# A decoder trunk on one core: the order of work in the state-space scan stage

## The reference

```
lam_bar = exp(lam * dt); b_bar = ((lam_bar - 1) / lam) * (b_re + i b_im)   # 32 groups, 64 states, 16 channels
bu = einsum('bsgc,gpc->bsgp', u, b_bar)
h  = scan over time of  h[t] = lam_bar * h[t-1] + bu[t]
y  = einsum('bsgp,gcp->bsgc', h, c).real + d_skip * u;  y = gelu(y)
compress(z, j): blocks of 32 tokens (stride 16) of z + cmp_pos[j], gelu(zb @ cmp_w1[j] + cmp_b1[j]) @ cmp_w2[j]
```

## Time and profile before

| | |
|---|---|
| median of 3 runs | 1891.24 us |
| profiled execution | 1887.98 us, span 1886.2 us |
| PE busy | 1795.3 us (95%) |
| DVE, ACT, POOL busy | 926.4, 660.6, 182.2 us |
| end of a2_1 on PE, layer 1 | 70.52 us |
| end of POOL's table, layer 1 | 84.0 us |
| first L691 of batches 0 to 3, layer 1 | 118.80, 138.63, 160.30, 177.16 us |
| the same, layer 2 | 1050.70, 1070.49, 1092.50, 1109.32 us |
| DVE, per batch | blocks 1.5, `input_mats` 4.2, `output_mats` 4.6, skips 0.3, scan 5.9 us |
| DVE, hidden gelu with its tanh | 103.71 to 105.88 us, the three operations ahead of the tanh 1.3 us |
| `load_z2(0, 1)`, the first group | issued from 55.08 to 57.64 us |

### The profile page before, as it was taken

The page is one execution under the profiler, slowest core; times in us unless marked ns, Lnnn a source line. Parts: engine busy times, 40 slices in busy tenths (PEclk is TensorE's granted clock), DMA queues, the critical chain, the costliest instruction groups (busy, mean ns, idle before and its releaser), DMA issues.

```text
span 1886.2 us, 25936 instructions
## 1 busy us (share of the span) xinstructions
PE 1795.3 (95%) x9640; PEld 1440.8 (76%) x9640; DVE 926.4 (49%) x1465; ACT 660.6 (35%) x1156; POOL 182.2 (10%) x325
## 2 busy tenths in 40 slices
PE   6899999999989999999988999999999899999997
PEld 6677766778877888888766777767788688888886
DVE  4786576444444444422348956754443444444223
ACT  4332655522234222221253235654222432222112
POOL 3601060000000000000044010600000000000000
PEclk9999999999999999999999999999999999999999
DMA  7334112123222333322243341211333133333222
GB/s 259 103 99 110 57 51 62 58 89 100 89 74 74 98 94 98 98 90 90 79 171 94 107 106 55 62 35 56 90 93 97 56 94 96 100 94 96 90 89 78
DMA packets 65590, 171.11 MB, mean 91 GB/s; under 512 B 14480, under 2 KB 26768, under 8 KB 64736
## 3 DMA queue, kind: packets, MB, share of 16 engines
q1 hardware_dynamic: 40192, 140.53, 24.2%
q10 hardware_dynamic: 22208, 14.16, 2.9%
q0 software_dynamic: 3104, 15.25, 2.6%
HBM read 160.18 MB, written 7.08 MB: 89 GB/s over the span
## 4 chain that ended last, share of the span: by engine, by line
PE 83%; DVE 8%; ACT 4%; DVEq 3%; issue 1%; DMA 1%; ACTq 0%
PE ps L503 18%; PE ps L505 17%; PE ps L504 17%; PE ps L542 6%; PE ps L544 5%; PE ps L543 5%; PE ps L759 2%; PE ps L772 2%; PE ps L785 2%; PE ps L533 1%; DVE ta L1266 1%; DVE wlo L1260 1%; PE ps L641 1%; ACT rta L929 1%; DMA xt<-xin 1%
## 5 line engine op out<-in xcount | busy, mean ns | idle before, releaser
L503 PE MATMUL ps<-xh,whi 128*128 128x512 f32 x1312 | 523.3, 399 | 18.7 <-DVE wlo L1260 11.5
L505 PE MATMUL ps<-xh,wlo 128*128 128x512 f32 x1312 | 514.5, 392 | 0.0
L504 PE MATMUL ps<-xl,whi 128*128 128x512 f32 x1312 | 514.2, 392 | 0.0
L1260 DVE TENSOR_TENSOR wlo<-raw,whi 128x1024 fp32r<-128x1024 f32 x264 | 328.4, 1244 | 340.8 <-ACT whi L901 331.1
L901 ACT ACTIVATE whi<-raw 128x1024 fp32r<-128x1024 f32 x264 | 278.1, 1053 | 369.3 <-PE ps L544 246.8
L503 PEld LDWEIGHTS ps<-xh,whi 128*128 128x128 f32 x1312 | 248.6, 190 | 72.3 <-DVE wlo L1260 13.2
L505 PEld LDWEIGHTS ps<-xh,wlo 128*128 128x128 f32 x1312 | 248.3, 189 | 53.2
L504 PEld LDWEIGHTS ps<-xl,whi 128*128 128x128 f32 x1312 | 248.8, 190 | 49.6
L542 PE MATMUL ps<-whi,hh 128*128 128x512 f32 x352 | 137.7, 391 | 5.1 <-DVE wlo L1260 5.1
L544 PE MATMUL ps<-whi,hl 128*128 128x512 f32 x352 | 137.1, 389 | 0.0
L543 PE MATMUL ps<-wlo,hh 128*128 128x512 f32 x352 | 137.0, 389 | 0.0
(11 more groups left out here) (338 smaller groups left out, 2437.7 us busy)
## 6 DMA issues: line engine op xcount, KB each, us to landing
raw<-wstream SPq DMA_DIRECT2D x264, 512.0 KB, 3.5
w<-w1s POOLq DMA_DIRECT2D x4, 2048.0 KB, 12.3
sm<-smalls POOLq DMA_DIRECT2D x2, 1084.0 KB, 5.4
xt<-xin ACTq DMA_DIRECT2D x4, 512.0 KB, 10.6
scratch_u<-pa ACTq DMA_DIRECT2D x8, 256.0 KB
toep<-scratch_k ACTq DMA_DIRECT2D x4, 512.0 KB
scratch_y<-y ACTq DMA_DIRECT2D x8, 256.0 KB
toep_b<-scratch_k ACTq DMA_DIRECT2D x4, 512.0 KB
```

The costliest lines, as they stand in the source:

```text
L503: pe.matmul(ps[:, bank, :], wh, hi[:, k, :], start=first and i == 0, stop=False)
L504: pe.matmul(ps[:, bank, :], wh, lo[:, k, :], start=False, stop=False)
L505: m = pe.matmul(ps[:, bank, :], wl, hi[:, k, :], start=False, stop=last and i == len(blocks) - 1)
L1260: dve.tensor_tensor(wlo[:, c % 2, :], raw[:, c % 2, :], whi[:, c % 2, :].bitcast(f32), SUB).then_inc(lo_ready, 1)
```

## The change

`bch` holds the input blocks of all four batches (it lies where `gqt` was), made once by `input_blocks`; `skip` holds all skip matrices, made once. `s5_mats` is split on PE and ACT into the turn (`vmat` to `vt`) and the kernels (`bch`, `wmat` to `kam`), with a semaphore `vmat_ready` of its own; the turn of batch j+1 goes ahead, while the kernels of batch j+1 come after `s5_outputs(j)` and a slab, and are followed by one slab before `s5_outputs(j+1)`. PE does a2_3 and the hidden turns before the first turn and kernels. DVE adds the positions before it makes any matrix; ACT issues the second `load_z2` before `a2_out(0)`, and each split ahead of the stores and loads of u. The same matmuls are done in both kernels.

```diff
-    bch = more("bch", [P, 2, 4, SC])
+    bch = place("bch", at, [P, 2, GP, SC])          # at gqt
-    skip = place("skip", ys_at + 1024, [SC, 8, SC])
+    skip = place("skip", ys_at + 1024, [SC, SG, SC])
# PE
-                def s5_mats(b, j):
+                def s5_turn(b, j):
                     if j:
-                        pe.wait_ge(ka_copied, b)
-                    pe.wait_ge(mats_ready[j % 2], l * 2 + (j // 2 + 1))
+                        pe.wait_ge(vt_ready, b)
+                    pe.wait_ge(vmat_ready, b + 1)
...
+                def s5_kernels(b, j):
+                    if j:
+                        pe.wait_ge(ka_copied, b)
+                    pe.wait_ge(mats_ready[j % 2], l * 2 + (j // 2 + 1))
...
-                pe.wait_ge(vtok_ready, l + 1)
-                s5_mats(l * 4, 0)
+                a2_slab(3)
                 pe.wait_ge(qgate_tanh, l + 1)
                 pe.wait_ge(hid_copied, l + 1)
-                a2_slab(3)
                 for i in range(2):                    # hidden turns, L712
...
+                s5_turn(l * 4, 0)
+                pe.wait_ge(vtok_ready, l + 1)
+                s5_kernels(l * 4, 0)
                 b1_slab(0)
...
                 s5_states(l * 4, 0)
+                s5_turn(l * 4 + 1, 1)
                 b1_slab(1)
-                s5_mats(l * 4 + 1, 1)
                 for j in range(3):
                     s5_outputs(l * 4 + j, j)
+                    b1_slab(2 * j + 2)
+                    s5_kernels(l * 4 + j + 1, j + 1)
                     s5_states(l * 4 + j + 1, j + 1)
-                    b1_slab(2 * j + 2)
                     if j < 2:
+                        s5_turn(l * 4 + j + 2, j + 2)
                         b1_slab(2 * j + 3)
-                        s5_mats(l * 4 + j + 2, j + 2)
# ACT
                 a2_split(0)
+                load_z2(1, 0)
                 a2_out(0)
+                a2_split(1)
                 store_u(0)
-                load_z2(1, 0)
-                a2_split(1)
...
                 a2_out(1)
+                a2_split(2)
                 load_u(0)
                 store_u(1)
-                a2_split(2)
                 a2_out(2)
+                a2_split(3)
                 load_u(1)
                 store_u(2)
-                a2_split(3)
...
                 a2_out(3)
-                load_u(2); store_u(3); b1_split(1); store_k(l * 4, 0)
                 act.wait_ge(hid_psum, l + 1)          # bias
...
+                b1_split(1)
+                s5_turned(l * 4)
                 act.wait_ge(gelu_arg, l * 5 + 1)      # tanh
...
-                load_u(3); load_toep(l * 4, 0)
+                s5_kernels(l * 4); load_u(2); store_u(3); store_k(l * 4, 0)
                 b1_out(0)
                 b1_split(2)
+                load_toep(l * 4, 0); s5_turned(l * 4 + 1); load_u(3)
                 b1_out(1)
                 b1_split(3)
-                s5_mats(l * 4 + 1); store_k(l * 4 + 1, 1)
                 for j in range(3):
                     s5_outputs(b, j)
                     store_y(b, j)
-                    load_toep(b + 1, j + 1)
                     if j < 2:
                         b1_out(2 * j + 2)
                         b1_split(2 * j + 4)
+                    else:
+                        query_out(0, OQ0, 0)
+                        split_hi(hl_, OQ0 + 2)
+                    s5_kernels(b + 1)
+                    store_k(b + 1, j + 1)
+                    if j < 2:
+                        s5_turned(b + 2)
+                    load_toep(b + 1, j + 1)
+                    if j < 2:
                         b1_out(2 * j + 3)
                         b1_split(2 * j + 5)
-                        s5_mats(b + 2); store_k(b + 2, j + 2)
-                query_out(0, OQ0, 0)
-                split_hi(hl_, OQ0 + 2)
# DVE
+                def input_blocks():                   # all 16 columns of coef at once
+                    t1, t2 = ta[:, 0:256]..., tb[:, 0:256]...
+                    cmul(bch[:, 0, :, :], bch[:, 1, :, :], bc(coef[:, 0, :], 2, SC), bc(coef[:, 1, :], 2, SC), ...)
...
                 a2_lo(0)
-                input_mats(l * 4, 0)
+                add_positions(1)
                 a2_lo(1)
-                gq ...; for j in (1, 0): positions
+                add_positions(0)
                 a2_lo(2)
+                gq ...
+                input_blocks()
+                input_mats(l * 4, 0)
                 output_mats(l * 4, 0)
                 a2_lo(3)
-                skips(0); add_skip(l * 4); input_mats(l * 4 + 1, 1)
+                hidden_gelu()                         # with skips() ahead of its wait for the tanh
+                add_skip(l * 4, 0)
                 b1_lo(1)
-                gelu(...); output_mats(l * 4 + 1, 1)
+                input_mats(l * 4 + 1, 1)
+                scan(l * 4, 0)
...
                 b1_lo(2)
-                scan(l * 4, 0); b1_lo(3); input_mats(l * 4 + 2, 2); skips(1); add_skip(l * 4 + 1); output_mats(l * 4 + 2, 2)
                 for j in range(3):
+                    output_mats(l * 4 + j + 1, j + 1)
+                    b1_lo(2 * j + 3)
+                    if j < 2:
+                        input_mats(l * 4 + j + 2, j + 2)
+                    add_skip(l * 4 + j + 1, j + 1)
+                    b1_lo(2 * j + 4)
                     scan(l * 4 + j + 1, j + 1)
-                    b1_lo(2 * j + 4)
-                    if j == 0: input_mats(l * 4 + 3, 3)
-                    if j == 1: output_mats(l * 4 + 3, 3)
-                    if j < 2: b1_lo(2 * j + 5); skips(j + 2); add_skip(l * 4 + j + 2)
```

More of the change, by code:

```diff
@@ L1025, in load_u, with s5_turned @@
                     act.dma_start(u8s[i][:, :, :], scr_u[i].rearrange("c g t n -> t (c g) n")).then_inc(u8_in[i], 16)
[L1027 removed]
+                def s5_turned(b):
                     act.wait_ge(vt_psum, b + 1)
@@ L1030, in s5_mats, with s5_kernels @@
                        .then_inc(vt_ready, 1)
+                def s5_kernels(b):
                     act.wait_ge(ka_psum, b + 1)
@@ L1114, in _ @@
                 x.then_inc(hid_biased, 1)
+                b1_split(1)
+                s5_turned(l * 4)
                 act.wait_ge(gelu_arg, l * 5 + 1)
                 act.activation(hgt[:, :, :], hgt[:, :, :], ACT.Tanh, scale=GELU_B).then_inc(gelu_tanh, 1)
-                load_u(3)
-                load_toep(l * 4, 0)
+                s5_kernels(l * 4)
+                load_u(2)
+                store_u(3)
+                act.wait_ge(k_zeroed, 64)
+                store_k(l * 4, 0)
                 b1_out(0)
                 b1_split(2)
+                load_toep(l * 4, 0)
+                s5_turned(l * 4 + 1)
+                load_u(3)
                 b1_out(1)
                 b1_split(3)
-                s5_mats(l * 4 + 1)
-                store_k(l * 4 + 1, 1)
                 for j in range(3):
@@ L1521, in _ @@
                     x.then_inc(z_ready, 1)
+                a2_lo(0)
+                add_positions(1)
+                a2_lo(1)
+                add_positions(0)
                 a2_lo(2)
+                dve.wait_ge(qgate_tanh, l + 1)
+                dve.tensor_scalar(gq[:, :, :].rearrange("p t c -> p (t c)"), gq[:, :, :].rearrange("p t c -> p (t c)"), 1.0, 0.5, ADD, MUL)
+                input_blocks()
+                input_mats(l * 4, 0)
                 output_mats(l * 4, 0)
                 a2_lo(3)
-                skips(0)
-                add_skip(l * 4)
-                input_mats(l * 4 + 1, 1)
                 def b1_lo(i):
@@ L1553, in scan, with hidden_gelu @@
                           [x.rearrange(v3, g=4) for x in temps]).then_inc(h_ready, 1)
+                def hidden_gelu():
+                    y, t = hid[:, :, :], hgt[:, :, :]
+                    dve.wait_ge(hid_biased, l + 1)
+                    tt(t, y, y, MUL)
+                    dve.drain()
+                    dve.tensor_scalar(t, t, GELU_A, 1.0, MUL, ADD)
+                    dve.drain()
+                    tt(t, t, y, MUL).then_inc(gelu_arg, 1)
+                    skips()
+                    dve.wait_ge(gelu_tanh, l * 5 + 1)
+                    dve.scalar_tensor_tensor(t, t, 1.0, y, ADD, MUL).then_inc(hid_ready, 1)
+                hidden_gelu()
+                add_skip(l * 4, 0)
                 b1_lo(1)
-                dve.wait_ge(hid_biased, l + 1)
-                gelu(hid[:, :, :], hgt[:, :, :], l * 5).then_inc(hid_ready, 1)
-                output_mats(l * 4 + 1, 1)
+                input_mats(l * 4 + 1, 1)
+                scan(l * 4, 0)
                 dve.wait_ge(kc_psum, l + 1)
@@ L1567, in _ @@
                 b1_lo(2)
-                scan(l * 4, 0)
-                b1_lo(3)
-                input_mats(l * 4 + 2, 2)
-                skips(1)
-                add_skip(l * 4 + 1)
-                output_mats(l * 4 + 2, 2)
-                for j in range(3):
-                    scan(l * 4 + j + 1, j + 1)
-                    b1_lo(2 * j + 4)
-                    if j == 0:
```

(11 more changed lines are left out.)

50 lines of the change are left out of this document (15 added, 35 removed).

## The result

The changed kernel takes 1925.9 us (median of 4 runs, 1924.6 to 1928.5), the kernel before 1890.6 in the same job (4 runs, 1888.0 to 1892.6): ratio 1.0188, 95% interval [1.0174, 1.0201]. The prediction was 1881.4, range 1871 to 1896. It was wrong in sign and outside its range. The profiled execution took 1924.6 us with a span of 1922.8, against 1886.2 before.

What follows compares the result with a forecast made beforehand. PE, busy 95% of the span, bounds the kernel, so only its stalls count: 28.1 us removed less 18.2 of new waits gives 9.9 gained, 1878.1 from the profiled run, named as 1881.4 us; range 1871 to 1896 (8 in 10).

Steps and rivals of the forecast that it cites:

- the front: Start of the scan stage: position sums and z2 earlier remove the 4.9 us `wlo` wait and half clock, 7.5 us.
- the hidden products: Front of the stage: hidden matmuls follow the third slab at 76.1 us, their sums ready by about 73.2, so no stall.
- the first kernels: Ahead of the first kernels: a new wait of 1.1 us for output matrices that DVE ends at 91.3.
- the sum of removed stalls: PE's waits and half clock in the scan stage: 13.9 us in layer 1, 14.2 in layer 2, 28.1 in all.
- the first outputs: First output group L691 of layer 1: expected to start near 108 us instead of 118.8.
- 0.5 for the turn: Before the loop: PE asks for input_mats(1) at 100.6, DVE ends it at 101.1; a 0.5 us wait (0 to 1.5).
- 0.3 for kc: Ahead of the first outputs: scan and kc end at 108.0, PE comes free at 107.8; a 0.3 us wait.
- the mechanism of the loop: Batches 1 to 3: the Toeplitz chain through DRAM ends after PE reaches the outputs, 2.4 us wait three times per layer.
- 1.46 + 2.6: Toeplitz chain after the kernels end: the store is issued 1.46 us later and lands in 2.6, then the load starts.
- I take 6.0: Toeplitz load of 512 KB: assumed to land in 6.0 us, between bounds of 3.5 and 9.7.
- the new waits: Scan stage, per layer: 1.1+0.5+0.3+3x2.4 = 9.1 us, both layers 18.2.
- rival (b): Ahead of L691, batches 1 to 3: waits from about 3 us lower the clock, 1.5 us more each; 1897, chance 0.16.

Runs made afterwards that it cites:

- e5_kernels_earlier: Changed kernel with the kernels of batch j+1 put ahead of the slab and of outputs j; 1863.2 us, ratio 0.9857 to the kernel before.
- e6_half_load: Changed kernel loading half the rows of every Toeplitz block (512 instead of 1024), each used twice, so half the data is left out; 1888.0 us, ratio 0.9984.
- e7_raw_later: Changed kernel with DVE's low-part split of block 2j+4 behind the scan of batch j+1, so the raw load starts later; 1921.2 us, ratio 1.0164.
- e1_front_only: Changed kernel with its front kept and the batch loop in the order of before, kernels one batch ahead; 1882.2 us, ratio 0.9973.
- e9_front_scan_first: e1_front_only with the scan of batch 0 moved ahead of the output matrices of batch 1 on DVE; 1887.1 us, ratio 0.9986.
- e2_filled_wait: Changed kernel with 18 large matmuls, results unread, filling PE's wait ahead of outputs 1 to 3; 1900.5 us, ratio 1.0056.
- e3_wait_then_slab: Changed kernel with the wait for Toeplitz load and scan ahead of slab 2j+2, and the outputs behind that slab; 1926.0 us, ratio 1.0195.
- e8_small_fill: Changed kernel with 34 small matmuls of the outputs' size, results thrown away, ahead of outputs 1, 2 and 3; 1921.1 us, ratio 1.0172.

## Why the prediction was wrong

**Right: the front.** The third slab has no wait and a full clock; the hidden products start at 76.35 (predicted 76.1, before 83.72); the first kernels wait 1.40 for `wmat` (predicted 1.1); the `upool`, `wmat_b`, `pa` and scan waits are gone. `e5_kernels_earlier` bears out the sum of removed stalls. Off by a little: the first outputs start at 109.23, not 108; in place of 0.5 for the turn and 0.3 for kc there is one wait of 1.40 for the first Toeplitz load (2.81 in layer 2). The sum had followed that load nowhere: its store was issued at 96.87, right behind a u store of 256 KB, and landed only as the load went out, at 102.61.

**Right: the mechanism of the loop.** The chain kernels, copy, skip sum, store, load became the last thing that the outputs wait for, and the first half of its working held: the kernels of batch 1 end at T = 120.61, where the states begin, PE is free for outputs 1 at T+7.65 (predicted 7.75) and starts them at T+11.77, and the load was issued at T+3.9 (predicted 1.46 + 2.6 = 4.1).

**Wrong: "I take 6.0" for the load.** It takes 7.1 to 7.8 us. I priced the bytes at the 169 GB/s of the earlier trace rows, a window that lies behind the y store as well, and added 2.0 us from a store of 64 KB. `e6_half_load` puts the load's own bytes at 105 to 114 GB/s and the rest at 2.8 to 2.9 us, and `e7_raw_later` shows that the raw load beside it counts for 0.4 us on average. The waits were 3.9 to 4.1 in layer 1 instead of 2.4. With the waits ahead of outputs 0 the new waits are 14.9 us in layer 1 and 15.2 in layer 2, where the sum had 9.1 each: 11.9 us too few.

**Wrong, and larger: the clock behind the waits.** The sum has no term for it, and rival (b), whose mechanism it is, priced it at 1.5 us per wait and "from about 3 us on", from one slab. Behind outputs it is half of 11.5, 10.2 and 13.3 us in layer 1 and half of 10.2, 10.0, 10.2 and 13.4 in layer 2: 17.5 + 21.9 = 39.4 us. Filling six of the seven waits gave 25.4 of it back, net of what it did to the clock elsewhere. Slower had a chance of 0.17 and rival (b) a time of 1897; its condition, store and load together above 9.3 us, was met (122.14 to 132.38 is 10.2). That rival named the place and the direction, but took the price of a wait from matmuls of 512 columns, where 4 us at 0.62 were all of it, and carried it to groups of 64 columns, where it was 10 to 14 us at 0.50.

**The account.** Predicted 9.9 us faster, measured 36.6 slower by the spans: 46.5 us apart. The two terms make 11.9 + 39.4 = 51.3, 4.8 too much. A stretch at half clock loses a little less than half (3.3 us for 48 matmuls that took 7.2), which is 1.8 less over seven of them. PE's waits outside the stage are 2.7 us shorter than before. The granted clock outside the two stages differs little in sum: half of the time at half clock there is 13.7 us before and 15.3 after, although single stretches come and go, as the last section shows. So less than 2 us stay unexplained.

## What to carry to other kernels

Before an order is tightened, add up the longest chain through DRAM with a load timed in its own form (its rows, not its bytes) and with the transfers that will run beside it, and put at least that much of other matmuls between its two ends on TensorE. Here the chain took 11.8 us from the end of the kernels, and 7.7 us of other matmuls were not enough; the 16.9 to 24.4 us of `e5_kernels_earlier` were.

Price a wait of TensorE by what follows it, and as a risk. Ahead of the many small matmuls of the outputs even 1.25 us was followed by half clock in one execution, while 1.84 us in the kernel before was not. A wait that can't be avoided was cheaper ahead of a dense slab, or filled.

When several producers feed an engine that is 95% busy, move the late producer ahead of just enough other work, and leave the consumer where it is. `e5_kernels_earlier` uses the same instructions as the changed kernel and is 63 us faster; with the kernels a whole batch ahead (`e1_front_only`, `e9_front_scan_first`) another engine came to owe PE two things at once.

## What was not expected of the hardware

The same wait, of the same code, with two outcomes. Before, it ends at 391.88, with 0.62 over the next 4 us. After:

```profile
408.21 0.49 PE L503 MATMUL ps<-glh,whi 128*128 128x512 f32 x1 [3.21 <-DVE gll L1731]
```

```profile
408.00:412.00 4.00, 3.79 (x17) 3.15 (x18) 1.28 (x2) 0.06 (x1) 0.00 (x0) 1.00 0.27 77
```

The length of a wait alone does not decide it. Ahead of outputs 0 the kernel before waited longer than several of the waits that lost the clock, and kept it at 1.00 in both layers (1.84 and 1.70 us):

```profile
118.80 1.97 PE L691 MATMUL ps<-u,toep 128*128 128x64 f32 x16 [1.84 <-issue]
```

The 1.40 us ahead of outputs 0 of the changed kernel kept it too, and so did 2.56 ahead of a slab; 1.25 ahead of outputs 3 of `e6_half_load` and 1.97 in `e2_filled_wait` lost it. What decides between these was not tested, and stays open.

That a gap ahead of small matmuls is the costly place rests on the stretches behind outputs 1 to 3 here, against those behind the slabs in `e3_wait_then_slab`. It is not the kind of work alone: behind the short waits of `e6_half_load`, ahead of the same outputs, four of six stretches lasted 6.8 us. And 48 small matmuls in a row neither lowered a full clock (`e8_small_fill`) nor raised a low one: it came back only after the slab behind them had begun.
